# Moving the weight remainders of the attention stages from VectorE to GpSimd

## The reference

```python
for l in range(2):                                   # first block
    x = x + 0.5 * swiglu(rmsnorm(x, g_ffn1[l]), w_ffn1_gu[l], w_ffn1_down[l])
    z = rmsnorm(x, g_mix[l]) @ w_mix_in[l]
    # zb, zc, zv: y_conv = zb * causal_conv3(zc * zv); q, k, v, f: forgetting attention, 8 heads of 64
    x = x + concat(rmsnorm(y_conv), rmsnorm(y_att)) @ w_mix_out[l]
    x = x + memory_cross_attention(rmsnorm(x), rmsnorm(mem), w_xq[l], w_xkv[l], w_xo[l])   # 4 heads of 256
    x = x + 0.5 * swiglu(rmsnorm(x, g_ffn2[l]), w_ffn2_gu[l], w_ffn2_down[l])
x = rmsnorm(x, g_final)
x = diff_layer(x)         # differential attention: softmax(q1 k1) - lam * softmax(q2 k2), 8 heads, gated
x = stick_breaking(x)     # 16 heads of 64; weights from a suffix sum of log(1 - sigmoid(z)), gated
```

## Time and profile before

| | |
|---|---|
| runs, us | 3009.92, 3011.43, 3016.04 (median 3011.43) |
| the profiled execution, us | 3009.92 |
| its span, us | 3007.9 |
| granted TensorE clock, mean | 0.99 |
| PE / PE weight load / DVE / ACT / POOL busy | 97% / 81% / 54% / 36% / 13% |
| read from memory | 252.79 MB |

### The profile page before, as it was taken

The page is one execution under the profiler, slowest core; times in us unless marked ns, Lnnn a source line. Parts: engine busy times, 40 slices in busy tenths (PEclk is TensorE's granted clock), DMA queues, the critical chain, the costliest instruction groups (busy, mean ns, idle before and its releaser), DMA issues.

```text
span 3007.9 us, 35873 instructions
## 1 busy us (share of the span) xinstructions
PE 2914.5 (97%) x14832; PEld 2428.5 (81%) x14832; DVE 1617.9 (54%) x2239; ACT 1070.4 (36%) x1664; POOL 391.7 (13%) x262
## 2 busy tenths in 40 slices
PE   7999999899999999999999999999999999999999
PEld 6888888789888888888888779888888787777777
DVE  5554356565455533554346575555533666656664
ACT  3322234344333322332334344332323444343442
POOL 2000111120100001000111120100002211143430
PEclk9999999999999999999999999999999999999999
DMA  4332232133233232332232133232322211122211
GB/s 129 98 98 91 92 93 64 50 119 107 83 98 98 88 105 95 98 98 95 89 91 71 57 106 106 91 107 92 100 94 86 64 57 57 57 67 64 61 56 49
DMA packets 301361, 257.20 MB, mean 86 GB/s; under 512 B 10871, under 2 KB 299536, under 8 KB 301200
## 3 DMA queue, kind: packets, MB, share of 16 engines
q1 hardware_dynamic: 300880, 254.90, 27.3%
q0 software_dynamic: 320, 0.03, 0.0%
HBM read 252.79 MB, written 2.10 MB: 85 GB/s over the span
## 4 chain that ended last, share of the span: by engine, by line
PE 89%; DVE 6%; ACT 2%; issue 2%; POOL 1%; DMA 1%; SPq 0%; DVEq 0%; ACTq 0%; POOLq 0%
PE PS L1414 28%; PE PS L1416 27%; PE PS L1415 27%; PE PS L1420 2%; PE PS L1656 2%; DVE WL L2116 1%; DVE AF L2531 1%; ACT WH L1769 1%; PE PS L1661 1%; PE PS L1503 1%; PE PS L1612 0%; DVE AR L2538 0%; DVE SM L2449 0%; POOL SC L2641 0%; PE PS L1662 0%
## 5 line engine op out<-in xcount | busy, mean ns | idle before, releaser
L2116 DVE TENSOR_TENSOR WL<-RAW,WH 128x1024 fp32r<-128x1024 f32 x480 | 618.1, 1293 | 587.4 <-ACT WH L1769 585.8
L1414 PE MATMUL PS<-XH,WL 128*128 128x512 f32 x2256 | 902.0, 400 | 14.4 <-issue 9.0
L1416 PE MATMUL PS<-XH,WH 128*128 128x512 f32 x2256 | 884.6, 392 | 0.0
L1415 PE MATMUL PS<-XL,WH 128*128 128x512 f32 x2256 | 883.2, 391 | 0.0
L1769 ACT ACTIVATE WH<-RAW 128x1024 fp32r<-128x1024 f32 x448 | 465.5, 1043 | 1024.5 <-PE PS L1416 997.4
L1414 PEld LDWEIGHTS PS<-XH,WL 128*128 128x128 f32 x2256 | 426.9, 189 | 96.3 <-issue 15.6
L1416 PEld LDWEIGHTS PS<-XH,WH 128*128 128x128 f32 x2256 | 426.0, 189 | 91.6
L1415 PEld LDWEIGHTS PS<-XL,WH 128*128 128x128 f32 x2256 | 427.3, 189 | 81.8 <-issue 0.2
L1414 PE MATMUL PS<-AR,WL 128*128 128x512 f32 (+1 forms) x1216 | 466.3, 383 | 19.1 <-DVE AR L2361 7.5
L1416 PE MATMUL PS<-AR,WH 128*128 128x512 f32 (+1 forms) x1216 | 461.9, 380 | 0.0
L1415 PE MATMUL PS<-AR,WH 128*128 128x512 f32 (+1 forms) x1216 | 461.5, 380 | 0.0
(11 more groups left out here) (244 smaller groups left out, 3069.9 us busy)
## 6 DMA issues: line engine op xcount, KB each, us to landing
RAW<-in_w_ffn_gu_dram SPq DMA_DIRECT2D x176, 512.0 KB, 3.5
RAW<-in_w_ffn_down_dram SPq DMA_DIRECT2D x80, 512.0 KB, 3.4
RAW<-in_w_mix_in_dram SPq DMA_DIRECT2D x48, 512.0 KB, 3.8
RAW<-in_w_xkv_dram SPq DMA_DIRECT2D x32, 512.0 KB, 3.4
RAW<-in_a_w_in_dram SPq DMA_DIRECT2D x32, 512.0 KB, 4.0
RAW<-in_w_mix_out_dram SPq DMA_DIRECT2D x16, 512.0 KB, 3.5
RAW<-in_w_xq_dram SPq DMA_DIRECT2D x16, 512.0 KB, 3.4
RAW<-in_w_xo_dram SPq DMA_DIRECT2D x16, 512.0 KB, 3.3
```

What stands on the lines that cost most here:

```text
L1414: pe.matmul(o, ll, rh, start=start, stop=False, skip_group_check=skip)
L1415: pe.matmul(o, lh, rl, start=False, stop=False, skip_group_check=skip)
L1416: return pe.matmul(o, lh, rh, start=False, stop=stop, skip_group_check=skip)
L2116: dve.tensor_tensor(l, raw_slot(n), F(h), ALU.subtract).then_inc(sg["wl"].up(n))
```

## The change

`on_dve(n)` decides which engine computes the remainder of unit n. Before, DVE had all but the two padded units (kind `pad`), which GpSimd had. After, DVE keeps the units of the FFN stages and those units of the last stage that carry a gain and are not k weights. All others go to GpSimd: those of the mixers, the cross attentions and the differential layer, and in the last stage the k weights and the output weights. The semaphore that the users wait for (`wl` or `wp`) follows. The list of steps is otherwise unchanged.

```diff
     def on_dve(self, n):
-        return self.units[n][3] == "w"
+        key, _, gain, kind = self.units[n]
+        if gain is not None:
+            return key[0][1][0] != "k"
+        return kind == "w" and STAGES[key[0][0]].startswith("ffn")
```

## The result

The changed kernel takes 3030.56 us (median; 3024.14 to 3034.51) against 3012.22 us (3009.92 to 3016.04) for the kernel before in the same runs: the ratio is 1.0057, 95% interval 1.0034 to 1.0081. That is slower, by 10 to 24 us, and outside the predicted range of 3001 to 3027 us. It is near the 3029 us of rival (a), but not all by that rival's mechanism, as will be seen.

The account below looks back on a forecast made before the run. TensorE, busy 97% of the span, was taken as the bound. Terms 3.0 + 1.5 - 4.9 + 2.5 - 2.0 + 2.0 = +2.1 us on 3009.92 gave 3012, or 3013 against the median; range 3001 to 3027.

Parts of the forecast that it names:

- rival (a): POOL's in-order queue: remainders and sums of squares lengthen each other; +18 us, 3029; chance 0.34 together with rival (c).
- the head of the differential layer, "+1.5": Start of the differential layer: v1 remainders queue behind seven sums of squares, delaying v1's matmuls and first scores; +1.5 us.
- allow +2 in all: Small DVE steps in attention: locks mostly hidden by 4.7 us of slack; +2 us allowed where slack is less.
- 1.7 us of clock at the cross attention's start: Cross attention start: the low-clock stretch behind 3.21 us of PE idling goes away, winning 1.7 us.
- End of each mixer, "4.4 and 4.1 later": Mixer ends: remainders delay POOL's power and the next one locks out DVE's copy; PE 4.4 and 4.1 us later.
- a wait of 4 us or more for the copy: Sign at a mixer's end: PE's wait grows from 0.9 to 4 us or more, released by DVE's copy.
- Start of each cross attention, "the delay is swallowed": Cross attention start: PE's 4.4 us lateness shrinks to 1.0, clock wins 1.7, then q0 remainders and root cost 2.2.
- Middle of the differential layer, "-4.9": Middle of the differential layer: shorter DVE queue removes waits on L2416 (-3.9 us) and one before a copy (-1.0).
- End, "+2.5 to +3.5; I take 2.5": End of the differential layer: the remainder on POOL stands behind sums of squares; +2.5 to +3.5 us, 2.5 taken.
- Last stage, "-2": Last stage: two moved remainders stood right before what PE waited for; -1.0 us for each.
- the price: One remainder on POOL at 128x1024: 2.4 us, bounds 1.9 and 3.3.
- rival (c): Attention steps have too little slack: 25 locks cost 0.5 us each, +12, 3024; chance 0.34 together with rival (a).

Follow-up runs that it names:

- v1_back: Changed kernel with the two v1 units of the differential layer back on DVE; ratio to the kernel before 1.0043.
- head_back: Changed kernel with the first eight remainders of the differential layer (units 410 to 417) back on DVE; ratio to the kernel before 1.0034.
- best1: Kernel before with only the differential layer's remainders 420 to 448 and the last stage's from 456 on POOL; 2993.11 us, ratio 0.9935.
- mx_mid: Kernel before with 106 of the 128 mixer and cross attention remainders on POOL, without those at the turns; ratio 1.0004.
- one_unit: Kernel before with only unit 449, the last remainder of the differential layer, on POOL; ratio 1.0008.
- sb_only: Kernel before with only the changed kernel's 16 units of the last stage on POOL; ratio 1.0015.
- all_pool: All 480 remainders on POOL, the padded ones too; ratio to the kernel before 1.0034.
- sb_tail: Kernel before with only the last stage's 34 remainders from g0 (unit 456) on, q, g and v included, on POOL; ratio 0.9958.
- best2: As best1, with the two v0 remainders of each cross attention also on POOL; ratio to the kernel before 0.9942.

## Why the prediction was wrong, point by point

**The step that failed most: the head of the differential layer, "+1.5".** It was +9.7, 3.9 as waits of PE and 5.8 as slower matmuls. I stepped through POOL's queue for v1 only and put v1's remainders "behind the seven sums of squares". They are there (L2628 at 2332.12, 5.12 us for two), and v1_back shows that they are worth 1.8. I left out the next two pairs: k1 and q1 at 2345.86, and g0 and k2 at 2361.21. The latter lock L2457 just when the first exponentials need it. I had the lock, and had an "allow +2 in all" for small DVE steps; I took the slack of 4.7 us from a step of the mixer and carried it to a place that I had named as having less. Shown are the waits: v1_back gives back 1.8 us, and the wait for the first exponentials, 2.5 us in the changed kernel, stays at 2.2 in head_back and goes to 0.5 in best1. The slower matmuls that come with them are not shown unit by unit.

**The clock, charged at one wait per layer and moved, not added.** Of the 17.5 us of longer span, 12.8 are slower matmuls. I wrote of the 1.7 us of clock at the cross attention's start: "Such a stretch now falls behind the mixer's longer wait (it is in the 1.0) and goes away here". It did not go away: the granted clock is at the lower level twice, behind the wait of 2.11 us at the end of mix_0 and again behind the one of 2.39 us at the start of x_0. Windows of the changed kernel:

```profile
622.00:626.00 4.00, 4.00 (x10) 3.13 (x11) 0.00 (x0) 1.79 (x2) 4.00 (x2) 0.50 0.58 181
656.00:662.00 6.00, 5.55 (x18) 4.59 (x18) 1.43 (x3) 1.41 (x2) 6.00 (x4) 0.50 0.37 117
```

I gave no clock to new waits of 1.7 to 2.6 us in the head (clock 0.92 over 110 us) and to the end (0.89 over 31.7 us). One profile can be off by as much (mx_mid's has 10.6 us more and no slower median; one_unit's shows a stretch moved), but the executions together are not: the changed kernel's five have a granted clock of 0.981 to 0.985, the 64 of the kernel before 0.985 to 0.993. So the lower clock goes with the change. The median is slower by 18 us while PE idles 4.7 us more, so most of the loss is clock; which wait brings how much of it stays open.

**End of each mixer, "4.4 and 4.1 later": the lock was right, the wait only in one of two.** The rows of the changed kernel at the end of mix_0:

```profile
619.44 7.00 POOL L2628 TENSOR_TENSOR WL<-RAW,WH 128x1024 fp32r<-128x1024 f32 x3 [15.08 <-ACT WH L1772]
621.84 0.79 PE L1417 MATMUL PS<-AR,WL 128*128 128x512 f32 x1 [2.11 <-POOL WL L2628]
626.41 1.02 POOL L2686 TENSOR_TENSOR SM<-SM 128x4 f32<-128x4 f32 x1
627.40 2.38 POOL L2628 TENSOR_TENSOR WL<-RAW,WH 128x1024 fp32r<-128x1024 f32 x1
627.46 2.61 DVE L2370 COPY SC<-SM 128x512 f32<-128x512 f32 x1 [7.53 <-POOL SM L2686]
...
630.21 0.60 PE L1423 MATMUL PS<-IDR,SC 128*128 128x128 f32 x4
```

Three remainders, the power at 626.41 (I had its end at 625.8), at once the next stage's first remainder, and the copy locked beside it, 2.61 us where it took 0.43. PE's transposes come at 630.21, 5.9 later than before; 0.9 of that was there when the mixer began, so 5.0 for 4.4 predicted. But PE does not wait for the copy here. What I missed is the first of the three, o1's, for which PE waits 2.11 us; behind it the matmuls run at the lower clock, and PE reaches the transposes 0.1 us after the copy's end, so that either alone would have held them until about then. The sign I had named, a wait of 4 us or more for the copy, is missing: there is none in mix_0 and one of 2.6 us in mix_1, the L2370 of the waits above.

**Start of each cross attention, "the delay is swallowed": half.** I had PE catch up 3.4 us, win 1.7 of clock and lose 2.2 at q0, -2.9 for the stage. Measured are -0.9 and -2.3 us for the stages. The last sum comes at 655.6 and not at 653. The waits for it fell to 2.4 and 1.6 us, not under 1, and the low clock behind the first cost what the shorter wait won: x_0 idles 1.8 us less and is 0.9 shorter. Mixer and cross attention together cost 6.1 us in two layers for +3.0 predicted.

**Middle of the differential layer, "-4.9": right,** -5.7 in the window, 4.0 of it idle time, with the waits on L2416 nearly gone as said. **End, "+2.5 to +3.5; I take 2.5": the wait is right,** 4.4 us for 1.8; with the clock the end is 5.3 longer.

**Last stage, "-2": wrong sign.** It was +1.4, and sb_only alone +4.4. I counted the remainders that leave DVE and not which one stays where PE waits: k leaves, those of q, g and v stay before L2541, and now begin behind POOL's product. The waits for it went from 12.8 us to 13.4 and the longest from 2.8 to 4.5. In all PE idles only 0.6 us more in this stage (28.4 for 27.8): what is shown is that the 2.0 us were not won, more than that there was a loss.

**A reading that was wrong.** "All idle time lies in the six stages whose weight remainders move": they hold 76.1 of the 93.4 us. The other 17.3 lie before mix_0, at the program's start, and the change does not reach them.

**Right:** the price, 2.4 predicted and 2427 ns measured; the FFN windows; the full cover in the middle of mixers and cross attentions (mx_mid), and in the FFN stages behind mix_0 even with everything moved (all_pool); the lock as one means of harm. With mx_mid at 1.0004, rival (c), a loss of 12 us from locks in the steady part, falls too.

**Rival (a)** gave nearly the right time, partly by luck: it has the price of a remainder at 3.3 us and sums of squares that hold each other up; the price stayed 2.43, the seven sums took 10.38 us for 12.07, and PE waited less for the sums. Its own sign, a last sum over 3 us later than I had it, is just missed (655.6 for 653). Its name, POOL's in-order queue, is right, its place is not.

## What to carry to other kernels

In these runs, work that is moved from DVE to POOL is free in the steady part of a stage and dear at its turns: list every moved instruction near a turn with its start and end in the receiving queue, and ask of each which tiny step of the other engine falls into it; a 0.16 us step took 1.87 us beside one. In the last stage here, moving nearly all remainders out of the queue that PE waits for won 12 us of 3014 (sb_tail), and moving only some won nothing: what stays behind can change which engine gets in first. Count a new wait of PE as more than its length where the clock falls behind it, as behind the 2.11 us at the end of mix_0, but don't book the clock wait by wait.

## What the runs showed that I had not expected

A DVE step on two elements per partition is held until POOL's subtraction ends, just as a copy of 128x512 is: 1.87 us for 0.16. And the stretching is large in sum, 112 us of DVE for 184 remainders and 349 us for all of them, while nearly all of it stays hidden: PE idles 4.7 and 4.9 us more. One sum must be watched with care: idle of PE and time do not go in step. best2 idles least of all (3.2 us less than best1) and its profiled matmuls took 11.5 us longer, at a granted clock of 0.986 against 0.990; its ratio is no better. And all remainders on POOL, 480 in one group with 1151.3 us of work, hurt no more than 184 (1.0034 against 1.0057).
